# Two blocks of a one-core kernel: norms through per-token sums, linear units side by side, and the inverse's steps between parts of units

## The reference

```python
def first_block(x, c, w_ada, ...):
    ada = c_act @ w_ada[l] + b_ada[l]
    sh1, sc1, g1, sh2, sc2, g2 = jnp.split(ada, 6, axis=-1)
    h = modulate(rmsnorm(x, norm1_g[l]), sh1, sc1)
    z = h @ w_in[l]
    ...
    y = jnp.concatenate([head_rmsnorm(y_a, ...), head_rmsnorm(y_b, ...)], axis=-1) @ w_out[l]
    x = x + g1[:, None, :] * y
    h = modulate(rmsnorm(x, norm2_g[l]), sh2, sc2)
    x = x + g2[:, None, :] * peer(h, w_q[l], sub_keys[l], expert_u[l], expert_v[l])
    return rmsnorm(x, final_g)

def gated_delta_rule(q, k, v, g, beta):
    q = l2_normalize(q) * (dk ** -0.5)
    k = l2_normalize(k)
    gc = jnp.cumsum(g, axis=-1)
    a = jnp.where(strict, (k * beta) @ k.T * decay, 0.0)
    t_inv = triangular_solve(a + eye, eye)
    u = t_inv @ (v * beta)
    w = t_inv @ (k_beta * jnp.exp(gc))
    ...
    # scan over chunks: v_new = u - w @ S; o = q_dec @ S + intra @ v_new; S = S * gl + k_dec.T @ v_new
```

## Time and profile before

| What | us |
|---|---|
| median of 3 runs (lowest, highest) | 1967.79 (1965.06, 1971.36) |
| the profiled execution | 1973.12 |
| its span, first to last instruction | 1971.4 |
| first block to the first expert unit | 0 to about 342 |
| experts and final norm | 342 to 1528 |
| second block | 1528 to 1971.4 |

### The profile page before, as it was taken

How to read it: one execution, slowest core, us unless ns; L and a number is a source line. 1 busy time by engine, 2 the same in 40 slices (tenths; PEclk the granted TensorE clock), 3 DMA queues, 4 the chain that set the end, 5 groups by cost and what they waited for, 6 DMA issues and landing times.

```text
span 1971.4 us, 28772 instructions
## 1 busy us (share of the span) xinstructions
PE 1835.6 (93%) x10239; PEld 1584.9 (80%) x10239; DVE 1579.6 (80%) x2571; ACT 703.5 (36%) x1121; POOL 1046.6 (53%) x649
## 2 busy tenths in 40 slices
PE   6998869999999999999999999999999998988885
PEld 4776747999999899999978887878887676766764
DVE  5975867968989798888489999999997968757656
ACT  2342232433333344444333333333333433224441
POOL 1332225478888655565567666666764552344001
PEclk7998879999999999999999999999999999999888
DMA  8241332489999879988899999999995121200011
GB/s 346 88 166 59 131 147 75 134 300 314 312 315 305 279 262 317 312 294 306 305 361 352 356 352 354 355 353 350 364 355 202 57 96 54 75 22 3 1 56 51
DMA packets 159917, 440.47 MB, mean 223 GB/s; under 512 B 13648, under 2 KB 62928, under 8 KB 156752
## 3 DMA queue, kind: packets, MB, share of 16 engines
q1 hardware_dynamic: 64400, 254.71, 36.9%
q0 software_dynamic: 36864, 134.23, 18.2%
q10 hardware_dynamic: 58560, 50.34, 7.8%
HBM read 386.80 MB, written 52.43 MB: 223 GB/s over the span
## 4 chain that ended last, share of the span: by engine, by line
PE 70%; DVE 15%; issue 5%; POOL 4%; ACT 3%; DMA 2%; ACTq 0%; DVEq 0%; SPq 0%; PEldq 0%; POOLq 0%
PE PS L940 33%; PE PS L1147 25%; PE PS L1110 4%; POOL w_lo L832 3%; DVE arena L1784 1%; DVE arena L1975 1%; PE PS L1182 1%; ACT w_hi L1361 1%; PE PS L955 1%; DVE arena L1743 1%; PE PS L1173 1%; POOL arena L881 1%; PE PS L994 1%; DMA xres<-in_x 1%; DMA arena<-in_expert_u_rows,arena 1%
## 5 line engine op out<-in xcount | busy, mean ns | idle before, releaser
L832 POOL TENSOR_TENSOR w_lo<-raw,w_hi 128x1024 fp32r<-128x1024 f32 x300 | 723.8, 2413 | 795.0 <-ACT w_hi L1361 749.8
L1361 ACT ACTIVATE w_hi<-raw 128x1024 fp32r<-128x1024 f32 x332 | 351.9, 1060 | 989.3 <-PE PS L940 631.2
L940 PE MATMUL PS<-act_hi,w_hi 128*128 128x384 f32 (+1 forms) x1632 | 602.9, 369 | 29.7 <-DVE act_lo L1756 14.7
L940 PE MATMUL PS<-act_hi,w_lo 128*128 128x384 f32 (+1 forms) x1632 | 586.6, 359 | 0.0
L940 PE MATMUL PS<-act_lo,w_hi 128*128 128x384 f32 (+1 forms) x1632 | 586.3, 359 | 0.0
L940 PEld LDWEIGHTS PS<-act_hi,w_hi 128*128 128x128 f32 x1632 | 311.4, 191 | 78.7 <-issue 21.8
L940 PEld LDWEIGHTS PS<-act_lo,w_hi 128*128 128x128 f32 x1632 | 311.2, 191 | 25.7
L940 PEld LDWEIGHTS PS<-act_hi,w_lo 128*128 128x128 f32 x1632 | 311.9, 191 | 24.2 <-issue 1.4
L1147 PE MATMUL PS<-w_hi,act_hi 128*128 128x512 f32 x768 | 301.3, 392 | 5.5 <-ACT arena L1505 2.9
L1147 PE MATMUL PS<-w_lo,act_hi 128*128 128x512 f32 x768 | 300.1, 391 | 0.0
L1147 PE MATMUL PS<-w_hi,act_lo 128*128 128x512 f32 x768 | 300.0, 391 | 0.0
(11 more groups left out here) (330 smaller groups left out, 1901.9 us busy)
## 6 DMA issues: line engine op xcount, KB each, us to landing
raw<-in_expert_u SPq DMA_DIRECT2D x128, 512.0 KB
raw<-in_expert_v SPq DMA_DIRECT2D x128, 512.0 KB
raw<-in_w_in SPq DMA_DIRECT2D x52, 512.0 KB
arena<-in_w_ada SPq DMA_DIRECT2D x24, 1024.0 KB, 6.7
gel_d<-arena ACTq DMA_DIRECT2D x64, 384.0 KB
gates_d<-arena ACTq DMA_DIRECT2D x12, 2048.0 KB
arena<-gates_d SPq DMA_DIRECT2D x32, 768.0 KB, 7.2
arena<-gel_d SPq DMA_DIRECT2D x32, 768.0 KB
```

The costliest lines, as they stand in the source:

```text
L832: pool.tensor_tensor(w_lo[:, k % SPLIT, :], raw[:, k % RAW, :], w_hi[:, k % SPLIT, :].bitcast(F32), ALU.subtract).then_inc(lo_split, 1)
L940: mm = pe.matmul(PS[:, bank, 0:n_tok], w[:, k % SPLIT, c * P:(c + 1) * P], x[:, c, 0:n_tok], start=(i == 0 and n == 0), stop=(i == KC - 1 ...
L1361: act.activation(w_hi[:, k % SPLIT, :], raw[:, k % RAW, :], ACT.Copy).then_inc(hi_split, 1)
```

## The change

First block. The softplus of the recurrence's parameter moves to the start. The halves of `ada` come in the order 0, 2, 1, 3, so that chunks 0 to 3 of norm 1 have gain and shift after two halves; PE takes a share of one half instead of two. PE runs 36 matmuls on ones at the start. Norms 1 and 2 take sums for each token (`token_sums`), a root and reciprocal of 128x4 (`norm_root`, `norm_invert`), a copy 512 wide and four 128x128 matmuls (`norm_back`). The scaled operands go into PSUM. Units 0 and 1, U_OUT and U_OUT+1, U_Q and U_Q+1 run as pairs in two banks (`linear_pair`), chunk by chunk; the second U_OUT unit's `lower` is on DVE. Column sums of `ada` stand between chunks of a unit (`ADA_IN`), halves 6 and 7 are weighted at units 8 and 10. Head sums and spreads stand inside the next unit, behind its fifth chunk, and earlier.

Second block. q and k are squared at units 3 to 10 and summed for each token; roots at w = 6 and 10; eight spreads (ACT copy, four PE matmuls, DVE scale) at w = 8, 9, 10, 11, 12, 12, 13, 13. `cumulate` moves from 16 to 15, `rows` goes from DVE to ACT and with `products` and `decay` to w = 15 to 20. Units 21 to 31 are cut into four parts of six matmuls, and the 56 steps of the inverse stand between the parts. All 32 attention slots come behind unit 31 and the inverse, two for each step of the delta rule's chain.

```diff
+PARTS = 4
+INVERSE_FROM = 21
+ROWS_AT = (15, 17, 18, 19)
+DECAY_AT = (16, 17, 18, 20)
...
+    def inverse_steps():
+        done = [("mask", 0, 0), ("mask", 0, 1)]
+        for level in range(LEVELS):
+            for what, tb in (("M", 0), ("M", 1), ("X", 0), ("M", 2), ("X", 1), ("M", 3), ("X", 2), ("X", 3)):
+                done.append((what, level, tb))
+                if what == "M" and 4 * level + tb + 2 < 4 * (LEVELS - 1):
+                    done.append(("mask", level + (tb + 2) // 4, (tb + 2) % 4))
+        return done
+    inverse = inverse_steps()
+    share = len([st for st in inverse if st[0] != "mask"]) / (PARTS * (32 - INVERSE_FROM))
+    owed = 0.0
+    for w in range(32):
+        if w >= INVERSE_FROM:
+            for k in range(PARTS):
+                steps.append(("part", w, k))
+                owed += share
+                while inverse and (owed >= 1 or inverse[0][0] == "mask"):
+                    owed -= inverse[0][0] != "mask"
+                    steps.append(inverse.pop(0))
+        if 3 <= w < 11:
+            steps.append(("square", w - 3))
         steps.append(("unit", w))
         if 1 <= w <= 12:
             steps.append(("tanh", w - 1))
         if w <= 12:
             steps.append(("conv", w))
-        if 12 <= w < 20:
-            steps.append(("sum", w - 12))
+        if 3 <= w < 11:
+            steps.append(("sum", w - 3))
+        if w in (6, 10):
+            steps.append(("norm_root", w // 10))
+        for n, at in enumerate((8, 9, 10, 11, 12, 12, 13, 13)):
+            if at == w:
+                steps += [("spread", n), ("scale", n)]
         if w == 13:
             steps.append(("rates", 0))
         if w == 14:
             steps.append(("rates_turned", 0))
-        if w == 16:
+        if w == 15:
             steps.append(("cumulate", 0))
-        if 13 <= w <= 20:
-            steps.append(("scale", w - 13))
-        if w >= 20 and w % 2 == 0:
-            steps.append(("rows", w // 2 - 10))
-        if w >= 20 and w % 2 == 1:
-            steps.append(("products", w // 2 - 10))
-            steps.append(("decay", w // 2 - 10))
-    steps.append(("unit", 28))
-    fill = 29
-    steps += [("mask", 0, 0), ("mask", 0, 1)]
-    for level in range(LEVELS):
-        for what, tb in (("M", 0), ("M", 1), ("X", 0), ("M", 2), ("X", 1), ("M", 3), ("X", 2), ("X", 3)):
-            if (what, level) == ("X", 0):
-                steps.append((what, level, tb))
-            if what == "X":
-                if fill < 32:
-                    steps.append(("unit", fill))
-                elif fill == 32:
-                    steps += [("values", q) for q in range(TB)]
-                    attend()
-                elif not (level == 6 and tb % 2):
-                    attend()
-                fill += 1
-            if (what, level) != ("X", 0):
-                steps.append((what, level, tb))
-            if (what, level, tb) in (("X", 5, 1), ("X", 6, 1)):
-                steps.append(("tokens", level - 5))
-            if what == "M" and 4 * level + tb + 2 < 4 * (LEVELS - 1):
-                steps.append(("mask", level + (tb + 2) // 4, (tb + 2) % 4))
-    for kind, n in (("solve", 0), ("tokens", 2), ("solve", 1), ("read", 0), ("scan", 0), ("tokens", 3), ("solve", 2),
-                    ("read", 1), ("scan", 1), ("solve", 3), ("read", 2), ("scan", 2), ("read", 3), ("scan", 3)):
+        if w in ROWS_AT:
+            steps.append(("rows", ROWS_AT.index(w)))
+        if w in DECAY_AT:
+            steps.append(("products", DECAY_AT.index(w)))
+            steps.append(("decay", DECAY_AT.index(w)))
...
+    steps += inverse
+    steps += [("values", q) for q in range(TB)]
+    for kind, n in (("tokens", 0), ("tokens", 1), ("solve", 0), ("tokens", 2), ("solve", 1), ("read", 0), ("scan", 0),
+                    ("tokens", 3), ("solve", 2), ("read", 1), ("scan", 1), ("solve", 3), ("read", 2), ("scan", 2),
+                    ("read", 3), ("scan", 3)):
+        if (kind, n) != ("read", 0):
+            attend()
         steps.append((kind, n))
         if kind == "scan":
             steps.append(("gsquare", n))
             if n >= 2:
                 steps.append(("groot", n - 2))
-        if kind in ("tokens", "read", "scan"):
-            attend()
+        attend()
     steps.append(("gturn", 0))
     while len([st for st in steps if st[0] == "pv"]) < MH * TB // 2:
         attend()
...
-        PE_SHARE = (2, 3)
-        ADA_AFTER = {5: 4, 7: 5, U_OUT + 1: 6, U_OUT + 2: 7, U_OUT + 3: 8, U_OUT + 4: 9, U_Q + 2: 10, U_Q + 4: 11}
+        PE_SHARE = (2,)
+        ADA_IN = {6: 4, 8: 5, 12: 6, 14: 7, U_OUT + 4: 8, U_OUT + 6: 9, U_Q + 3: 10, U_Q + 5: 11}
+        WEIGHTED_AT = {8: 6, 10: 7, U_OUT + 2: 8, U_OUT + 4: 9}
         Y_ORDER = (0, 1, 4, 5, 6, 2, 7, 3)
-        Y_SQUARE = (11, 14, 15, 16, 17, 18, 19, 20)
-        Y_SUM = (12, 15, 16, 17, 18, 19, 20, 20)
-        Y_INV = (13, 16, 17, 18, 19, 20, 20, 20)
-        Y_SPREAD = (17, 18, 19, 20, 20, 20, 20, 20)
+        Y_SQUARE = (11, 14, 14, 15, 16, 17, 17, 20)
+        Y_SUM = (12, 15, 15, 16, 16, 17, 17, 20)
+        Y_INV = (13, 16, 16, 20, 20, 18, 18, 20)
+        Y_INV_FIRST = {17: (3, 4)}
+        Y_SPREAD = (16, 17, 17, 18, 18, 20, 20, 20)
+        FIRST_PAIR = ((0, 0), (0, 1), (1, 0), (0, 2), (1, 1), (0, 3), (1, 2), (1, 3),
+                      (0, 4), (0, 5), (1, 4), (0, 6), (1, 5), (0, 7), (1, 6), (1, 7))
+        NEXT_PAIR = ((0, 0), (0, 1), (1, 0), (0, 2), (1, 1), (0, 3), (1, 2), (0, 4), (1, 3),
+                     (0, 5), (1, 4), (0, 6), (1, 5), (0, 7), (1, 6), (1, 7))
...
+            def linear_pair(u, banks, steps, split, before=None):
+                last = [max(i for i, (e, _) in enumerate(steps) if e == n) for n in range(2)]
+                known = 0
+                for i, (e, c) in enumerate(steps):
+                    if before:
+                        before(i)
+                    if (e, c) == (e, 0):
+                        pe.wait_ge(*lowered(u + e))
+                    if c >= known:
+                        known = c + 1
+                        pe.wait_ge(alo_ready, split + known)
+                    at = Y_ORDER[c] if u == U_OUT else c
+                    for n, (w, x) in enumerate(((w_hi, act_hi), (w_lo, act_hi), (w_hi, act_lo))):
+                        mm = pe.matmul(PS[:, banks[e], :], w[:, (u + e) % SPLIT, at * P:(at + 1) * P], x[:, at, :],
+                                       start=(c == 0 and n == 0), stop=(c == KC - 1 and n == 2))
+                    if i == last[e]:
+                        mm.then_inc(unit_done, 1)
+            def token_sums(src, bank, start, stop):
+                for q in range(TB):
+                    mm = pe.matmul(PS[:, bank, q:q + 1], src[:, q * P:(q + 1) * P], ones[:, 0:1],
+                                   start=(start and q == 0), stop=stop, skip_group_check=True)
+                return mm
+            def norm_back(n, b):
+                pe.wait_ge(spread_ready, n)
+                for q in range(TB):
+                    mm = pe.matmul(PS[:, b, q * P:(q + 1) * P], tmp[:, 1, q * P:(q + 1) * P], ident[:, :],
+                                   start=True, stop=True)
+                mm.then_inc(spread_ps, 1)
...
-            squares(0, 8, 0, ones)
-            for h in range(4):
-                ada_half(h)
-            for u in range(U_OUT):
+            for n in range(36):
+                pe.matmul(PS[:, 7, 0:P], ones[:, :], ones[:, :], start=True, stop=True)
+            for c in range(8):
+                pe.wait_ge(sq_ready, c + 1)
+                mm = token_sums(sq[:, c % 2, :], 6, c == 0, c == 7)
+                mm.then_inc(sq_used, 1)
+            pe.wait_ge(sq_used, 8)
+            pe.nop().then_inc(sum_ready, 1)
+            ada_half(0)
+            norm_back(1, 7)
+            ada_half(1)
+            def rest_of_ada(i):
+                if i == 8:
+                    ada_half(2)
+                    ada_half(3)
+            def heads_of(u):
+                for i in range(8):
+                    if Y_SPREAD[i] == u:
+                        head_spread(i)
+                    if Y_SUM[i] == u:
+                        head_sum(i)
+            linear_pair(0, (0, 1), FIRST_PAIR, 0, rest_of_ada)
...
-            def scaled(n, src, gain):
-                v.scalar_tensor_tensor(out=tmp[:, n % 2, :], in0=src, scalar=gain, in1=rinv, op0=ALU.mult,
+            def scaled(n, src, gain, by):
+                v.scalar_tensor_tensor(out=PS[:, 3 + n % 2, :], in0=src, scalar=gain, in1=by, op0=ALU.mult,
...
+                if kind == "rows":
+                    act.wait_ge(rate_ready, 1)
+                    if tb:
+                        wait_full(act, "br", tb - 1)
+                    for h in range(GH):
+                        k = 4 * tb + h
+                        act.activation(h4(M1[:, 0, :])[:, h, :], upper[:, :], ACT.Copy, scale=rate[:, k:k + 1]).then_inc(rows_in, 1)
```

(6 more changed lines are left out.)

343 lines of the change are left out of this document (206 added, 137 removed).

## The result

The changed kernel took 2026.7 us (median of 4 runs, 2024.9 to 2028.6) against 1969.6 us before. The ratio is 1.029, with a 95% interval from 1.028 to 1.031. I had forecast 1966 us, with a range that ended at 1989 and a chance of 0.33 for slower. Direction and size were both wrong.

What follows compares the result with a forecast made beforehand. PE, busy for 93% of the span, was taken as the bound. First block -26 and second +24.5 us made 1973.1 into 1971.6, less 5.3 for the profiled execution: 1966 us, range 1941 to 1989.

Steps and rivals of the forecast that it cites:

- units 2 to 19: First block: waits and clock loss removed balance added sums, spreads and DVE's delay; 0 us, bounds -9 to +7.
- unit 19 to the end of U_OUT: First block, head norms and output projection: 79.2 us shrink to 54.9 us; -24.5 us, bounds -17 to -27.
- query projection, to the first expert unit: End of first block: running the two units as a pair saves time; -2.5 us, bounds 0 to -4.
- first block: Sum of the terms from the start to the query projection: -26 us, bounds -14 to -31.
- sums and spreads of q and k, with the clock: Second block, units 3 to 13: sums and exposed spreads cost +21 us, a lower clock +2 us.
- cumulate and rows: Second block: waits at w = 15 and for rows at w = 17 and 18; +4 us, bounds 0 to +7.
- inverse and attention: Second block: inverse costs 42 us under units, tail takes 92 us; -2.5 us, bounds -11 to +10.
- the pairs give nothing: Rival, first block: operands' pace sets both ends, so the block gives only 14 us; 1978 us, chance 0.11.
- Clock at q and k: Rival, units 8 to 13 and rows: waits hold the clock down, 15 us not 2; 1985 us, chance 0.19.
- Dense tail: Rival, second block's tail: attention's DVE work runs at 90% busy, tail takes 85 us; 1947 us, chance 0.28.
- a tail over 104 us: Sign of being wrong, second block: the tail, forecast at 92 us, lasting beyond its range's end.
- DVE beside POOL: Norm 2 and query projection: scaled operands reading PSUM never wait for POOL; query pair gains 2 us more, 1964 us.

Runs made afterwards that it cites:

- first_only: The changed kernel's first block with the second block left as before the change; 1959.6 us, 0.994 of before.
- norms_old_inverse: The changed kernel with only the second block's order of inverse and attention put back to that of before; 1997.4 us, 1.014 of before.
- copies_ahead: The changed kernel with only ACT's copy for each q and k spread moved ahead of the unit behind which the spread stands; 2001.0 us.
- norms_rows_back: The changed kernel with spread copies ahead, the old inverse and attention order, and cumulate, rows, products and decay in their old places; 1957.6 us, 0.994 of before.
- parts_2: The changed kernel with units 21 to 31 cut into 2 parts of 12 matmuls instead of 4 of 6; 2018.7 us.
- apart: The changed kernel with all 32 attention slots first in the tail and the delta rule's chain behind them; 2047.4 us, 1.040 of before.
- weighted_later: first_only with two of ada's halves weighted at units 13 and 16 instead of 8 and 10, their column sums moved along; 1982.8 us.

## Why the prediction was wrong, step by step

| Step | forecast, us | measured, us | from |
|---|---|---|---|
| start, to unit 2 | +2 | 0 | traces |
| units 2 to 19 | 0 | +4.4 | traces |
| unit 19 to the end of U_OUT | -24.5 | -20.5 | traces |
| norm 2 | -1 | 0 | traces |
| query projection, to the first expert unit | -2.5 | -1.1 | traces |
| first block | -26 | -17; -12 | traces; `first_only`, medians |
| sums and spreads of q and k, with the clock | +23 | +34 | traces |
| cumulate and rows | +4 | +7 to +8 | traces, before's six later sums taken off |
| inverse and attention | -2.5 | +24; +29 | traces; medians, against `norms_old_inverse` |
| output projection behind the tail | 0 | +2 | traces, clock 0.83 for 0.86 |

The profiled execution took 2025.6 us, 54 us over the 1971.6 that the terms had made; the median was then 1 us above it, not 5.3 below.

**First block.** The one large step was right in sign and near in size, 4 us short, and units 2 to 19 took another 4 us. The waits of 2.3 to 2.6 us behind pairs came as worked out. Units 2 to 19 lost the spreads' waits, as forecast, but two stretches of 24 matmuls still took 7.3 us. The delay by DVE's halves was 4.4 us, where I had put 7. (The windows from 144.6 to 210.1 us hold units 15 to 19, not 17 to 19 as I wrote.) By the medians the block gave 12 us, which is outside my bounds of -14 to -31. The rival "the pairs give nothing" was right as to the pairs; the gain came without them.

**Clock at q and k.** The mechanism was there as a rival, and its point of decision (a clock under 0.9) was met: 0.78. The term was mis-sized: +2 forecast, 12.6 measured (after against `copies_ahead`), and that rival's own price for these units, 15 us, was near. I had taken the row of a single wait of 3.20 us with a full clock behind it as the nearest, and not the window at 0.85 with a wait behind each unit, which was the true likeness: there too, short waits came one for each unit. Nor was the single wait a safe row. The one of 2.83 us behind unit 3 in after has a lower clock behind it:

```profile
1544.00:1553.00 9.00, 8.84 (x40) 7.42 (x41) 8.40 (x12) 2.69 (x5) 5.22 (x4) 0.81 0.40 117
```

The waits in front of the spreads were sized well for units 8 and 9 (1.44 us beside a sum), and for units 10 and 11 nearly (3.03 and 3.65 us, where 2.23 + 1.28 less a sum of 0.95, and 2.23 + 1.28, make 2.6 and 3.5).

**Cumulate and rows.** I had read the 4.63 us as a wait for `cumulate`; they stood at the sum ahead of it, behind the same chain. The wait at `cumulate` was sized well all the same, 6.01 us for 5.8, and those for the rows nearly, 3.56 us for 3.1, twice. With them goes the clock, 0.89, which the term had left out. And the comparison itself was the wrong one: in their old places, with no reciprocals of 3.35 us on DVE, both would have had nearly no wait, and the move cost 19 us [`norms_rows_back`].

**Inverse and attention.** This is the step that failed most: 26 us by the traces (31 by the medians, where some 5 us are the clock of the spreads). It had two parts.
- Under the units the inverse cost 115.5 - 11 x 5.46 = 55 us, not 42. What was left out is the longer first matmul of each part, 0.24 us for each of 41 returns, 10 us [after's timeline, `parts_2`]; the rest is the wait at the start, 3.70 us where I had 3 for all waits, and the low clock behind it.
- In the tail I held DVE's 76 us of work for the bound and divided by a busy share of 83%: 92 us. It took 117 us, with DVE busy for 61% of it. The slots alone show that DVE is busy for 58% and that a slot takes 2.65 us [`apart`]. The steps of the inverse had stood in waits that were there anyway. Taking out 49 of them shortened it, from the first logits to the last product, from 134.1 (`norms_old_inverse`) to 112.7 us, 0.4 us for a step, and its clock fell from 0.89 to 0.79.

These two errors, 13 and 25 us, make more than 26. Most of the difference is the 10 us of steps and wait that stood among units 29 to 31 before: the term counts all steps as new under the units and doesn't take the old ones off. That this slip went the other way is luck.

"Dense tail" was the rival that I gave 0.28; nothing of it came. Its counter-argument in the text, that DVE was never over 77% busy in that stretch, was the better reading: when an engine that is said to be the bound stands idle for a quarter of the time, look first for what it waits for. My own sign of being wrong, a tail over 104 us, came.

**Range.** The second block lost 70 us, against bounds of +5 to +46; even all four upper bounds together make only 56. The tail's end was at 104 us, and it took 117; no bound had the price of a part or the clock behind the early rows. So the failure is in the terms, not a bad draw within them.

**DVE beside POOL.** At norm 2, where one of the scaled operands had taken 2.73 us before, all eight now took 0.75 to 0.76 us. But this tests nothing: POOL didn't run there, from 257.9 to 278.3 us. The test came at norm 1, where two of them ran while POOL lowered a unit (POOL, then DVE):

```profile
27.96 4.67 POOL L845 TENSOR_TENSOR w_lo<-raw,w_hi 128x1024 fp32r<-128x1024 f32 x2 [23.83 <-ACT w_hi L1476]
31.67 1.42 DVE L1889 SCALAR_TENSOR_TENSOR PS<-xres,small,PS 128x512 f32<-128x512 f32 x2
```

They took 0.76 and 0.75 us; the first was wholly within POOL's operation. The rule of the Trainium skill that the prediction cites ("SBUF — State Buffer", "Who interferes with whom"), that a DVE instruction with at most one input in SBUF does not contend with GpSimd, agrees with this. The 2 us more that the prediction hung on it for the query projection didn't show: norm 2 and the projection together gained 1.1 us, not the forecast 3.5.

## What to carry to other kernels

Moving small steps from a stretch full of waits into a stretch where the engine is full makes each of them cost its whole length, and the stretch that they leave shrinks by much less: price both sides by a trace, 0.98 and 0.4 to 0.56 us here. A copy that one engine makes for the next belongs in its queue ahead of the work that waits for the current unit, since waits of 0.9 to 3.7 us behind every unit cost something again through TensorE's clock: 12.6 us on top of 15.3 us of waits in after, about half of that in `norms_old_inverse`. A step that is to be moved should be compared with its old place in the new kernel too, not with the old kernel alone. Before dividing work by a busy share, ask what the share says: DVE, held for the bound, was busy for 58 to 77% here, and the time went by a chain across engines. And moving a reader moves the release of its buffer, and with it what stands behind that buffer's transfer in the queue: 16.5 and 11.5 us in `weighted_later`.

## What was new about the hardware

- Waits of 1.4 to 3.7 us, one behind each unit, brought PE's granted clock down to 0.78 over 66 us: 50.9 us of PE time for what took 38.3 us at the upper level. The same eight waits gave 0.78 in four traces, 0.80 in one and 0.89 in one. A single wait of 2.83 us was followed by 9 us at 0.81, one of 3.20 us by a full clock. The attention alone ran at 0.58 with PE busy for 73% of the time, in small matmuls; work without use raised the tail's clock from 0.79 to 0.90.
- A return from 64x64 matmuls to 128x512 matmuls costs about 0.4 us in a stretch without waits: 0.25 us at the long matmuls, 0.15 at the small ones.
- A DVE operation with one input in SBUF and one in PSUM took 0.76 us within an operation of POOL, where one with two inputs in SBUF had taken 2.73 us.
